# Attention steps of a decoder layer: transposes of probabilities and of cached keys take turns in three banks, and the samples' three fills stand together

## The reference, cut to what matters

```
for window, dilation in ((128, 1), (512, 4), (2048, 16)):      # three branches per head
    s = q @ k^T * 64**-0.5 + relative_position_bias            # causal, strided keys
    p, lse = softmax(s)
    out_branch = p @ v
out = sum over branches of softmax(lse)[branch] * out_branch   # per token and head
```

## Time and profile before

| | |
|---|---|
| runs | 1950.23, 1951.59, 1954.95 us, median 1951.59 |
| the profiled execution | 1951.98 us, of it 1950.2 us span on the engines |
| TensorE's granted clock over the span | 0.991 |
| PE busy, share of the span | 97% |
| DVE, ACT, POOL busy | 52%, 24%, 26% |
| the 24 attention steps | about 320 to 655 us |

### The profile page before, as it was taken

One profiled execution on the slowest core, in us unless ns is written; L12 is line 12 of the kernel. 1 busy time (PEld: TensorE's weight loads), 2 busy tenths in 40 slices (PEclk: granted clock), 3 DMA queues, 4 the chain that ended last, 5 costly groups with the idle time before them and its releaser, 6 DMA issues.

```text
span 1950.2 us, 33054 instructions
## 1 busy us (share of the span) xinstructions
PE 1887.1 (97%) x13253; PEld 1753.8 (90%) x13253; DVE 1019.9 (52%) x2075; ACT 460.5 (24%) x926; POOL 515.0 (26%) x380
## 2 busy tenths in 40 slices
PE   6999998999999999999999999999999999999998
PEld 6999987777677899999659999999999999999997
DVE  6698816566666454511553374544544544544544
ACT  5100014666555521200441130001001001001005
POOL 2332322010100144453002223222222222222234
PEclk9999999999999999999999999999999999999998
DMA  5399967587767512123630132432432432411112
GB/s 156 132 317 340 333 215 221 161 255 228 201 195 244 190 44 76 55 87 128 207 109 26 48 118 90 172 129 86 172 129 87 174 135 104 153 43 43 43 32 92
DMA packets 220003, 281.36 MB, mean 144 GB/s; under 512 B 7522, under 2 KB 206570, under 8 KB 218154
## 3 DMA queue, kind: packets, MB, share of 16 engines
q1 hardware_dynamic: 219901, 279.94, 44.1%
HBM read 266.48 MB, written 113.89 MB: 195 GB/s over the span
## 4 chain that ended last, share of the span: by engine, by line
PE 88%; DVE 6%; SPq 2%; issue 1%; DMA 1%; ACT 1%; POOL 0%; DVEq 0%; POOLq 0%; ACTq 0%
PE bank L1570 26%; PE bank L1606 13%; PE bank L1091 9%; PE bank L1337 8%; PE bank L1354 5%; PE bank L1192 3%; PE bank L1149 3%; PE bank L1038 3%; PE bank L1182 2%; PE bank L1209 2%; PE bank L1317 2%; PE bank L1532 1%; PE bank L1238 1%; PE bank L1163 1%; SPq L656 1%
## 5 line engine op out<-in xcount | busy, mean ns | idle before, releaser
L929 POOL CAST w_hi<-w_raw 128x1024 fp32r<-128x1024 f32 x98 | 105.2, 1074 | 961.0 <-issue 325.7
L1570 PE MATMUL bank<-g_lo,w_hi 128*128 128x362 f32 (+1 forms) x1008 | 334.3, 332 | 0.0
L1570 PE MATMUL bank<-g_hi,w_lo 128*128 128x362 f32 (+1 forms) x1008 | 333.8, 331 | 0.0
L1570 PE MATMUL bank<-g_hi,w_hi 128*128 128x362 f32 (+1 forms) x1008 | 331.2, 329 | 0.0
L931 POOL TENSOR_TENSOR w_lo<-w_raw,w_hi 128x1024 fp32r<-128x1024 f32 x98 | 248.6, 2537 | 7.9
L2624 DVE TENSOR_TENSOR xT<-bank,xT 128x362 f32<-128x362 f32 (+1 forms) x264 | 141.4, 536 | 121.2 <-PE bank L1606 121.2
L1570 PEld LDWEIGHTS bank<-g_hi,w_lo 128*128 128x128 f32 x1008 | 191.4, 190 | 0.0
L1570 PEld LDWEIGHTS bank<-g_hi,w_hi 128*128 128x128 f32 x1008 | 190.0, 188 | 0.3 <-POOL w_lo L931 0.3
L1570 PEld LDWEIGHTS bank<-g_lo,w_hi 128*128 128x128 f32 x1008 | 189.7, 188 | 0.0
L1606 PE MATMUL bank<-act_lo,w_hi 128*128 128x362 f32 (+1 forms) x480 | 157.6, 328 | 0.0
L1606 PE MATMUL bank<-act_hi,w_hi 128*128 128x362 f32 (+1 forms) x480 | 157.6, 328 | 0.0
(11 more groups left out here) (304 smaller groups left out, 3856.5 us busy)
## 6 DMA issues: line engine op xcount, KB each, us to landing
out_sk_dram<-in_cache_win_k_dram SPq DMA_DIRECT2D x24, 2040.0 KB
out_sv_dram<-in_cache_win_v_dram SPq DMA_DIRECT2D x24, 2040.0 KB
kb<-in_cache_win_k_dram SPq DMA_DIRECT2D x48, 512.0 KB, 5.0
vn<-in_cache_win_v_dram SPq DMA_DIRECT2D x22, 1024.0 KB, 7.9
w_raw<-in_w_in_dram SPq DMA_DIRECT2D x22, 512.0 KB, 10.6
w_raw<-in_w_ffn_gate_dram SPq DMA_DIRECT2D x22, 512.0 KB, 3.8
w_raw<-in_w_ffn_up_dram SPq DMA_DIRECT2D x22, 512.0 KB, 3.8
w_raw<-in_w_ffn_down_dram SPq DMA_DIRECT2D x22, 512.0 KB, 3.7
```

The source lines that it names most:

```text
L929: pool.tensor_copy(w_hi[slot][:, :], w_raw[slot][:, :]).then_inc(w_hi_done, 1)
L1570: last = pe.matmul(out, w, r, start=start, stop=stop)
```

## The change

A function `first_fills(d)` lists the fills at the head of step d, and both the numbering and PE's program go by it. In an even step P and K0 take turns, P, K0, P, K0, P, K0, P, K0, P, and the three PS fills follow together. In an odd step K2 fills stand third and sixth: P, P, K2, P, P, K2, P. ACT copies in the same order; DVE's own order stays as it was. No instruction is added or taken away, and no copy changes its engine.

```diff
+        def first_fills(d):
+            u, second = divmod(d, 2)
+            if not d:
+                return [("K0", 0, i) for i in range(4)]
+            p = [("P", d - 1, i) for i in range(5)]
+            if second:
+                k = [("K2", u, i) for i in range(2)]
+                return p[0:2] + k[0:1] + p[2:4] + k[1:2] + p[4:5]
+            k = [("K0", u, i) for i in range(4)]
+            s = [("PS", u - 1, i) for i in range(3)]
+            return [p[0], k[0], p[1], k[1], p[2], k[2], p[3], k[3], p[4]] + s
+
         for d in range(STEPS):
             u, second = divmod(d, 2)
-            if d:
-                number("P", d - 1, 5)
+            for kind, at, i in first_fills(d):
+                FILL[kind, at, i] = len(FILL)
             if second:
-                number("K2", u, 2)
                 if u:
                     number("OS", u - 1, 1)
...
             else:
-
-                for i in range(4):
-                    FILL["K0", u, i] = len(FILL)
-                    if u and i < 3:
-                        FILL["PS", u - 1, i] = len(FILL)
...
-            def turn_p(d):
-
-                for i in range(5):
+            def turn_p(d, fills=range(5)):
+
+                for i in fills:
                     pe.wait_ge(ex_done, 4 * d + (3 if i < 2 else 4))
...
-                if d:
-                    turn_p(d - 1)
-                if second:
-                    turn_keys(u, 2, [0, 1])
-                else:
-                    for i in range(4):
-                        turn_keys(u, 0, [i])
-                        if u and i < 3:
-                            turn_sample_p(u - 1, [i])
+                for kind, at, i in first_fills(d):
+                    if kind == "P":
+                        turn_p(at, [i])
+                    elif kind == "PS":
+                        turn_sample_p(at, [i])
+                    else:
+                        turn_keys(at, int(kind[1]), [i])
                 scores(d)
...
-                if d:
+                if second:
+                    turned_p(d - 1, [0, 1])
+                    turned_last_keys(u, [0])
+                    turned_p(d - 1, [2, 3])
+                    turned_last_keys(u, [1])
+                    turned_p(d - 1, [4])
+                elif u:
                     turned_p(d - 1)
-                if second:
-                    turned_last_keys(u)
-                elif u:
                     turned_sample_p(u - 1)
```

More of the change, by code:

```diff
@@ L1727, in filled, with turned_p @@
                 return bank[4 + f % 3], t_free[f % 3]
-            def turned_p(d):
-                for i in range(5):
+            def turned_p(d, fills=range(5)):
+                for i in fills:
                     src, free = filled("P", d, i)
@@ L1735, in turned_p, with turned_last_keys @@
                     act.activation(p_T[:, 4 * i * P:4 * i * P + 512], src[:, :], ACT.Copy).then_inc(free, 1)
-            def turned_last_keys(u):
+            def turned_last_keys(u, fills):
                 if u:
                     act.wait_ge(st_ready, 3 * u)
-                for i in range(2):
+                for i in fills:
                     src, free = filled("K2", u, i)
```

## The result

Changed kernel: 1961.05 us, median of 11 runs (1950.26 to 1964.25). Kernel before, in runs beside it: 1950.23 us, median of 11 (1945.08 to 1956.88). Ratio 1.0051, 95% interval 1.0036 to 1.0066 (it compares all the runs and so differs a little from the ratio of the medians): half a per cent slower, 10.8 us by the medians, where the prediction said none. The profiled run took 1964.25 us, the longest of the eleven.

A forecast was written before the change was run, and what follows sets the result against it. PE's own sequence was taken to bound the kernel, its heads paced by the round through a bank. 0 - 4 x 0.3 + 0.7 + 0.85 = +0.35 us gave 1951.9 us against the median of 1951.59, range 1948 to 1956.

The forecast's parts named there:

- Even heads, 0: Heads of the 11 even steps 2 to 22: no gain; bounds a gain of 0.3 us and a loss of 0.15 each.
- the rule that spoke for a gain: PSUM emptying in even heads: using both ScalarE and VectorE would let the nine alternating fills go at PE's own pace.
- the first rival: Alternating copiers hide all PE's waits in even heads: 0.6 us each, 6.6 in all, total 1945.3 us; chance 0.08.
- Even heads with a = 0, -0.3 each: Steps 4, 8, 12, 16, 20: DVE is free sooner for the first scores, gaining 0.3 us a head, bounds 0.2 and 0.5.
- Odd heads, 0.06 each: Scores of odd steps start 0.06 us later; times 11 heads 0.7 us, bounds 0 and 1.1.
- the +0.35 of the sum: Whole kernel: even heads, a = 0 heads, odd heads and unit 10 together make it 0.35 us slower.
- unit 10's 0.85: Step 21's head: PE waits about 1.1 us for late K2 keys; 0.85 us lost, bounds 0.4 and 1.5.
- What else moves: Other engines: POOL's later refill of small rows and ACT's later end of the even head's copies cost nothing.
- a stall of PE's own supply: Earlier K2 loads fall onto the values' loads; two more stalls in heads or `values` add 7.1 us, 1959.0; chance 0.06.

The follow-up runs named there:

- even_only: Kernel before with the new order in even heads alone; step 4's scores to step 5's took 11.10 us, against 11.24 in the kernel before.
- after_strips_later: Changed kernel with the strips' loads issued behind the keys' load and second scores tile, and `w_out`'s tile 2 loaded later: 1952.03 us, 0.18% shorter than the kernel before.
- before_strips_later: Kernel before with the strips' loads issued behind the keys' load and the step's second scores tile: 1951.82 us, 0.15% shorter than the kernel before.
- before_early: Kernel before with the strips' loads issued two units earlier, in units 1 and 5; the changed kernel with the same move has a median 5.1 us above it.
- after_early: Changed kernel with the strips' loads issued two units earlier, in units 1 and 5: 1957.3 us, against 1955.8 for the kernel before.
- step7_only: Kernel before with the new order of an odd head's fills in step 7 alone: five runs from 1948.8 to 1953.5 us, seven from 1958.2 to 1966.2.

## Why the prediction was wrong

**Even heads, 0: right.** Step 18's head lasts 5.89 us as before, and the steps agree to 0.01 us. The rounds through a bank set the pace, whoever copies. So the rule that spoke for a gain, both engines emptying the banks, brought nothing here: the 6.6 us of the first rival did not come.

**Even heads with a = 0, -0.3 each: 0.13.** VectorE started on step 4's scores 0.64 us behind them in place of 0.78, and the keys' matmuls came at 2.44 in place of 2.57. even_only keeps this gain of 0.13; in the changed kernel the odd head that follows takes nearly all of it.

**Odd heads, 0.06 each: 0.11.** The sign stands; over 11 heads it is 1.2 in place of 0.7. With the heads of a = 0 the order itself costs 0.5 us, about the +0.35 of the sum. That the two come out so close is luck: the gain at a = 0 was put 0.6 us too high and the odd heads' loss 0.5 too low, and unit 10's 0.85, which follows, made up for both.

**Unit 10, +0.85: did not come.** The working took SyncE's times of before for those after. Counted back from step 21's scores, it was through with the early values 1.5 us sooner: it issued the last keys at 607.8 us, 8.7 us ahead of the scores and not 7.2.

**"What else moves": the step that failed.** It priced the engines and the queues by who waits for whom in the program. Two things outside that were left out. One is PE's supply, which was a rival ("a stall of PE's own supply") at 0.06. Its argument against was that PE's list has the same number of instructions and one such stall occurs in 24 steps. The number of instructions was beside the point: the page ends where it did, and what matters is the traffic ahead of its read. And the earlier trace rows was read as a one-off, when its place was that of the strips' loads, and step 7 has the same loads. Its price was wrong too: 3.56 us for a stall, where step 7 lost 7.26, since PE ran on at half clock. Step 15 could have shown it: with its 3.56 us it took 20.65 us, 5.4 more than step 7 without one. At 3.56 one more stall stood inside the range; at 7.26 it is 1959.2 us and outside. The mechanism I gave it, K2's loads falling onto the values' loads, is not what happened. The other is the collision of GpSimd's cast with VectorE's last group, 2.8 us, which was in no rival.

**Together.** By the profiles: 7.3 for step 7, 3.0 behind the attention, 0.5 for the order, 3.2 in stretches at half clock, less 0.5 in step 15, 0.3 in steps 0 and 1 and 1.4 ahead of the attention: 11.8 of 12.3 us. With the first two taken away (after_strips_later and before_strips_later) the medians of the two orders stand 0.2 us apart.

**What stays open.** Why the page of step 7 is read later when the head's last fill is one of probabilities: 3 us later without any strips, 4 to 6 us with them, in 10 profiles against 8 without an exception. It holds for step 7 alone. In step 15 the page is read 8.96 us behind the scores in the old order and 8.46 in the new one, and without strips 4.83 in before_early against 1.28 in after_early, the other way round. 256 records of PE back from the stalled matmul of step 7 lies the last fill of that head, 0.4 us ahead of the scores, so the border of the page that asks for the next one is near there; the same count from step 15's leads into its scores, which neither order changes. The last fill starts at the same time in both orders (its first weight load 0.60 us ahead of the scores in the old, 0.59 in the new), and both wait there for their bank. What differs in the records is the form: in the new order this wait is an instruction of its own, at 0.66 us ahead of the scores; in the old one it is part of the weight load, and the last wait with an instruction of its own stands at 1.10. Whether the page is asked for later by that, and so behind more of the strips, no run varied, and the request itself is not in the trace. What moved `w_out`'s landing by 0.4 us is open as well.

## What to carry to other kernels

A stall "for issue" in the middle of a run of matmuls, seen once, is worth locating before anything is priced: look at the instruction queue and at which loads stand ahead of it. Many loads of few long packets should not be issued where the next page is asked for; moving eight of them by 5 us took the stalls away, which no order of fills was seen to do in both steps. And a change that is worth nothing on the path can still cost by where it leaves two things that never met, here a cast and a group of subtractions.

## What the hardware showed that I had not expected

- A page of 16 KB that is normally read within 1 to 4 us of the same point was read up to 9.4 us behind it, and PE stood 1.7 to 4.5 us. Ahead of it stood 64 packets of 8224 bytes (0.66 us each by their records, 6.8 us from the first to the end of the last) and the keys' 1 KB packets, slowed from 0.05 to 0.12 us each; the 16 engines, busy throughout, moved 152 GB/s.
- The standstill is not the whole price: 4.24 us of it were followed by a granted clock of 0.63 over 6 us, and the step lost 7.26.
- VectorE's subtraction of two SBUF tiles beside GpSimd's took 1.37 and 2.67 us in place of 0.53; the other way round GpSimd's cast took 1.93 in place of 1.04.
- Whether a page is late seems to differ from run to run of one kernel: step7_only's twelve runs lie in two groups whose medians are some 10 us apart. Only one run of each kernel was profiled, so this is likely and not shown.
